# Expert weights of an encoder layer in one ring of fourteen 1 MB slots, loaded in order of use

## The reference

```python
h = h + memory_cross_attention(rms_norm(h, norm_cross[l]), mem_n, xa_wq[l], xa_wk[l], xa_wv[l], xa_wo[l])
h = h + hierarchical_moe(rms_norm(h, norm_ffn[l]), moe_router_group[l], moe_router_expert[l],
                         moe_w1[l], moe_w3[l], moe_w2[l])
return rms_norm(h, norm_final)

def expert_block(args):                     # for each expert, on the tokens routed to it
    xblk, e = args
    return (jax.nn.silu(xblk @ w1[e]) * (xblk @ w3[e])) @ w2[e]
```

## Time and profile before

| | us |
|---|---|
| median of 3 runs | 1872.28 |
| the profiled execution, its own time | 1873.4 |
| its span, first to last instruction | 1871.6 |
| PE busy in it | 1724.3 |

### The profile page before, as it was taken

How to read it: one execution, slowest core, us unless ns; L and a number is a source line. 1 busy time by engine, 2 the same in 40 slices (tenths; PEclk the granted TensorE clock), 3 DMA queues, 4 the chain that set the end, 5 groups by cost and what they waited for, 6 DMA issues and landing times.

```text
span 1871.6 us, 26055 instructions
## 1 busy us (share of the span) xinstructions
PE 1724.3 (92%) x10706; PEld 1088.5 (58%) x10706; DVE 840.5 (45%) x1165; ACT 522.3 (28%) x747; POOL 64.8 (3%) x33
## 2 busy tenths in 40 slices
PE   7989999999999999999799988899888898988996
PEld 7879899899777899978543332233323233232332
DVE  5566555798666454354643232232322323232233
ACT  5453443644354453344411000011000110000102
POOL 0004000033000000000000000000000000000001
PEclk9999999999999999999899999999999999999998
DMA  8753645444455565338499999999999999999995
GB/s 325 253 178 106 223 159 179 148 153 143 150 176 180 182 193 177 116 135 315 166 402 423 427 427 428 428 429 428 428 428 429 428 429 428 429 428 429 428 428 229
DMA packets 105393, 561.03 MB, mean 300 GB/s; under 512 B 9696, under 2 KB 9824, under 8 KB 79200
## 3 DMA queue, kind: packets, MB, share of 16 engines
q1 hardware_dynamic: 95808, 436.13, 59.7%
q10 hardware_dynamic: 9504, 123.74, 15.7%
HBM read 557.75 MB, written 2.10 MB: 299 GB/s over the span
## 4 chain that ended last, share of the span: by engine, by line
PE 67%; DMA 27%; DVE 3%; ACT 1%; issue 1%; SPq 0%; ACTq 0%; DVEq 0%
DMA arena<-in_moe_w_dram 27%; PE ps L970 14%; PE ps L617 7%; PE ps L619 6%; PE ps L618 6%; PE ps L611 6%; PE ps L612 6%; PE ps L613 6%; PE ps L1000 5%; PE ps L982 2%; PE ps L1017 2%; PE ps L916 1%; DVE w_lo L1575 1%; PE ps L858 1%; PE ps L839 1%
## 5 line engine op out<-in xcount | busy, mean ns | idle before, releaser
L970 PE MATMUL ps<-arena 128*64 128x512 f32 x2048 | 504.6, 627 | 84.1 <-DMA arena<-in_moe_w_dram 82.5
L1575 DVE TENSOR_TENSOR w_lo<-arena,w_hi 128x1024 fp32r<-128x1024 f32 x264 | 331.4, 1297 | 237.8 <-ACT w_hi L1145 237.6
L1145 ACT ACTIVATE w_hi<-arena 128x1024 fp32r<-128x1024 f32 x264 | 265.1, 1054 | 309.3 <-PE ps L613 169.4
L970 PEld LDWEIGHTS ps<-arena 128*64 128x64 f32 x2048 | 138.1, 142 | 346.4 <-issue 252.9
L2200 DVE TENSOR_TENSOR arena<-ps,arena 128x1024 f32<-128x1024 f32 x128 | 156.7, 1225 | 274.0 <-PE ps L1017 274.0
L1000 PE MATMUL ps<-arena 128*64 128x512 f32 x1024 | 225.6, 593 | 5.2 <-DVE arena L2177 3.2
L611 PE MATMUL ps<-x_hi,w_hi 128*128 128x256 f32 x512 | 148.4, 290 | 19.0 <-DVE w_lo L1575 19.0
L1000 PEld LDWEIGHTS ps<-arena 128*64 128x64 f32 x1024 | 73.2, 137 | 149.3 <-issue 139.5
L612 PE MATMUL ps<-x_lo,w_hi 128*128 128x256 f32 x512 | 147.5, 288 | 0.0
L613 PE MATMUL ps<-x_hi,w_lo 128*128 128x256 f32 x512 | 147.4, 288 | 0.0
L1430 ACT ACTIVATE arena<-ps 128x512 f32<-128x512 f32 x64 | 38.3, 599 | 385.3 <-PE ps L970 385.3
(11 more groups left out here) (363 smaller groups left out, 2409.7 us busy)
## 6 DMA issues: line engine op xcount, KB each, us to landing
arena<-in_moe_w_dram SPq DMA_DIRECT2D x133, 2048.0 KB, 20.1
arena<-in_moe_w_dram ACTq DMA_DIRECT2D x58, 2048.0 KB, 14.1
arena<-in_w_in_dram SPq DMA_DIRECT2D x52, 1024.0 KB, 5.1
arena<-in_xa_wk_dram SPq DMA_DIRECT2D x16, 1024.0 KB, 5.0
arena<-in_xa_wv_dram SPq DMA_DIRECT2D x16, 1024.0 KB, 5.0
arena<-in_w_out_dram SPq DMA_DIRECT2D x16, 1024.0 KB, 5.0
arena<-in_xa_wq_dram SPq DMA_DIRECT2D x16, 1024.0 KB, 5.0
arena<-in_xa_wo_dram SPq DMA_DIRECT2D x16, 1024.0 KB, 5.2
```

The source lines that it names most:

```text
L970: last = mm(ps[rows_, m, :], xe[par][:, ECH * i + c, :], ring_up[m][i][:, c, :], start=(i == 0 and c < 2), stop=(i == ECH - 1 and c >= 2))
L1145: fn(hi_ring[(2 * n + u) % 4][:], ring_a[i][:, 2 * u:2 * u + 2, :], ACT.Copy).then_inc(S["w_hi"], 1)
L1575: V.tensor_tensor(w_lo[i][:, 2 * u:2 * u + 2, :], ring_a[i][:, 2 * u:2 * u + 2, :], hi_ring[(2 * n + u) % 4][:].bitcast(F32), ALU.subtract ...
```

## The change

It replaces the three areas by one ring of 14 slots of 1 MB. `load_order` lists all 384 pieces in the order in which PE uses them; piece k goes to slot k mod 14 and waits only until piece k-14 is used. Two slots are new (`extra`, 16 KB of each partition; the scratch of the software DMA queue is cut to 1024 bytes to make room). All loads are of one piece, 8 KB for each partition, and all are on SP's queue; ACT issues none. Fourteen pieces can be loaded before the first is used: the 8 ups of expert 0, two ups of expert 1, the 4 downs of expert 0.

In the last column group of the output projection, PE finishes tokens 0 to 127 first (`last_stream`, `last_turn`, `last_logits`), and the add, squares, root and `hx_hi` of each half go on as soon as that half is there. `low_tokens` is cut finer. On PE two ups of expert 1 stand ahead of `slot_rows`, and the wait for the tables (`tab_dve`) goes to the end; the second half of the gather moves from experts 1 and 2 to experts 2 and 3. On DVE `tokens(1)` stands ahead of `select` of the second half and the tables. PE's and SP's loops over experts are written out. The core of the diff:

```diff
-RING_E = 3 * ECH
+UNIT = 1
+IN_PARTS = ()
...
+def load_order():
+
+    order = []
+    for n in range(NE + 1):
+        ups = [(n, m, i) for m in range(2) for i in range(0, ECH, UNIT)] if n < NE else []
+        downs = [(n - 1, 2, i) for i in range(0, ECH, UNIT)] if n else []
+        ahead = 2 // UNIT if 0 < n < NE - 2 else 0 if n else len(ups)
+        order += ups[:ahead] + downs + ups[ahead:]
+    return order
...
+        extra = Arena(sb("extra", [P, 16 * 256]))
...
-        ring_kib = [104, 112, 120, 128, 152, 160, 184, 192, 136, 144, 168, 176]
-        ring_up = [[arena(ring_kib[ECH * m + i], ECH, FF) for i in range(ECH)] for m in range(2)]
-        pair_up = [[arena(ring_kib[ECH * m + i], 2 * ECH, FF) for i in (0, 2)] for m in range(2)]
-        pair_dn = [arena(ring_kib[2 * ECH + i], 2, D) for i in (0, 2)]
-        ring_dn = [arena(ring_kib[2 * ECH + i], D) for i in range(ECH)]
+        slot_kib = [kib + 8 * k for kib in (104, 120, 152, 184, 202, 136, 168) for k in range(0, 2, UNIT)]
+        order = load_order()
+        unit_of = {unit: at for at, unit in enumerate(order)}
+        loads = [0] * len(slot_kib)
+        landed = []
+        for at in range(len(order)):
+            loads[at % len(slot_kib)] += 2 if at in IN_PARTS else 1
+            landed.append(loads[at % len(slot_kib)])
...
+
+        def slot_of(n, m, i):
+
+            first = i - i % UNIT
+            return unit_of[(n, m, first)] % len(slot_kib) if isinstance(n, int) and n < NE else over_slot[(m, first)]
+
+        def piece(n, m, i, many=1):
+
+            kib = slot_kib[slot_of(n, m, i)] + 8 * (i % UNIT)
+            home, kib = (arena, kib) if kib < 202 else (extra, kib - 202)
+            return home(kib, many * ECH, FF) if m < 2 else home(kib, many, D) if many > 1 else home(kib, D)
...
-            def load_up(e, n, m, i):
-
-                if not (isinstance(n, int) and n == 0):
-                    sp.wait_ge(S["up_used0" if m == 0 else "up_used1"], n * ECH + (i + 2 - ECH))
-                sp.dma_start(pair_up[m][i // 2], up_chunk(e, m, i)).then_inc(s_up[m][i // 2], 16)
-
-            def load_down(e, i):
-
-                sp.dma_start(pair_dn[i // 2], down_chunk(e, i)).then_inc(s_dn[i // 2], 16)
-
-            def load_expert(e, n):
-                for m in range(2):
-                    for i in range(0, ECH, 2):
-                        load_up(e, n, m, i)
+            used = ("up_used0", "up_used1", "dn_used")
+
+            def load_unit(at):
+
+                n, m, i = order[at]
+                parts, many = (2, 1) if at in IN_PARTS else (1, UNIT)
+                for k in range(parts):
+                    if at >= len(slot_kib):
+                        was_n, was_m, was_i = order[at - len(slot_kib)]
+                        sp.wait_ge(S[used[was_m]], was_n * ECH + was_i + (k + 1 if parts == 2 else UNIT))
+                    sp.dma_start(piece(n, m, i + k, many), expert_rows(n, m, i + k, many)).then_inc(s_slot[at % len(slot_kib)], 16)
...
             for m in range(2):
                 load_dense(G_XO + 2 + m)
-                for i in range(0, ECH, 2):
-                    load_up(0, 0, m, i)
+                for at in range(4 * m // UNIT, 4 * (m + 1) // UNIT):
+                    load_unit(at)
+            for at in range(8 // UNIT, 10 // UNIT):
+                load_unit(at)
...
+            def last_stream(j, i):
+
+                g, (a_hi, a_lo) = G_XO + 3, split[G_XO]
+                n_split, hi_ring = split_chunk(g, i)
+                o_, rows_ = ps[:, 2 * (g % 2) + j, :], slice(j * P, (j + 1) * P)
+                for c in range(CH):
+                    k, half = i * CH + c, 2 * n_split + c // 2
+                    if j == 0 and c % 2 == 0:
+                        pe.wait_ge(S["w_lo"], half + 1)
+                    hi, lo = hi_ring[half % 4][:, c % 2, :], w_lo[i][:, c, :]
+                    mm(o_, a_hi[:, k, rows_], hi, start=False, stop=False)
+                    mm(o_, a_hi[:, k, rows_], lo, start=False, stop=False)
+                    last = mm(o_, a_lo[:, k, rows_], hi, start=False, stop=(k == KT - 1))
+                if j == 1:
+                    last.then_inc(S["chunk_used"], 1)
+                elif i == NCH - 1:
+                    last.then_inc(S["xo_half"], 1)
+
+            def last_turn(j):
+
+                if j == 0:
+                    pe.wait_ge(S["proj_a"], act_evicts(G_XO + 4))
+                    pe.wait_ge(S["tp_act"], 3)
+                    pe.wait_ge(S["tp_dve"], 3)
+                else:
+                    pe.wait_ge(S["proj_b"], G_XO + 4)
+                for kk in (6, 7):
+                    for u in range(2):
+                        k = 2 * kk + u
+                        last = nc.tensor.transpose(bank(4 + kk % 2, 2, NT, P)[:, u, j, :], h[:, j, k * P:(k + 1) * P], ident)
...
-                dense_split(G_XO + n, False, split[G_XO], part=[2, 3])
-            group_turned(G_XO, 3, turn, 0)
-            logits(3)
-
-            pe.wait_ge(S["route_in"], 16)
+                if n < 3:
+                    dense_split(G_XO + n, False, split[G_XO], part=[2, 3])
+            last_stream(0, 2)
+            last_stream(0, 3)
+            last_stream(1, 2)
+            last_turn(0)
+            last_stream(1, 3)
+            last_logits(0)
+            last_turn(1)
+            last_logits(1)
...
+            up(1, 0, 0, 1)
+            up(1, 0, 1, 1)
             slot_rows()
-            pe.wait_ge(S["tab_dve"], 2)
-            block_n(1, 0, 1, (0, 1))
-            block_n(2, 1, 0, (2, 3))
-            block_n(3, 2, 1)
-            block_n(4, 3, 0)
-            block_n(5, 4, 1)
-            with pe.Fori(0, NE // 2 - 4) as e:
-                block_n(e * 2 + 6, e * 2 + 5, 0)
-                block_n(e * 2 + 7, e * 2 + 6, 1)
+            sums(0)
+            up(1, 0, 2, 1)
+            for i in range(ECH):
+                down(0, i)
+            up(1, 0, 3, 1)
+            for i in range(ECH):
+                up(1, 1, i, 1)
+                comb(0, i, 0)
+            for n in range(2, NE - 2):
+                block_n(n, n - 1, n % 2, {2: (0, 1), 3: (2, 3)}.get(n, ()))
             block_n(NE - 2, NE - 3, 0, behind=True)
             block_n(NE - 1, NE - 2, 1, behind=True)
             finish_n(NE - 1, 1)
+            pe.wait_ge(S["tab_dve"], 2)
...
+            act.wait_ge(S["proj_a"], act_evicts(G_XO + 4))
+            act.wait_ge(S["sq_part"], 6)
+            part_square(3, 0)
             sqrt_table()
-            rsqrt(NT)
-            act.wait_ge(S["rms_dve"], 2)
-            for j in range(NT):
-                fn(hx_hi[:, j], h[:, j, :].rearrange("p (q k) -> p k q", k=KT), ACT.Copy,
-                   scale=st[:, 40 + j:41 + j]).then_inc(S["hx_act"], 1)
+            root_of(0)
+            last_turned(0)
+            act.wait_ge(S["chunk_used"], (G_XO + 4) * NCH)
+            normalised(0)
+            act.wait_ge(S["proj_b"], G_XO + 4)
+            act.wait_ge(S["sq_part"], 7)
+            part_square(3, 1)
+            last_turned(1)
+            root_of(1)
+            normalised(1)
...
-            def down_hi(n, load):
-                for i in range(0, ECH, 2):
-                    act.wait_ge(S["dn_used"], n * ECH + i + 2)
-                    if load is not None:
-                        act.dma_start(pair_dn[i // 2], down_chunk(load, i)).then_inc(s_dn[i // 2], 16)
+            def down_hi(n):
+                act.wait_ge(S["dn_used"], n * ECH + ECH)
...
+            dve.wait_ge(S["xo_half"], 1)
+            last_add(0)
+            variance_of(0)
+            V.memset(lgrp, LOWEST)
+            last_turned(0)
+            inverse_of(0)
+            dve.wait_ge(S["chunk_used"], (G_XO + 4) * NCH)
+            last_add(1)
             V.memset(onesm, 1.0)
-            V.memset(lgrp, LOWEST)
-            dve.wait_ge(S["sq_part"], 8)
-            step(V.tensor_reduce(st[:, 0:NT], st[:, 44:52].rearrange("p (j g) -> p j g", g=4), AX.X, ALU.add))
-            rsqrt(NT, 1.0 / D)
-            V.tensor_copy(st[:, 40:42], st[:, 24:26]).then_inc(S["rms_dve"], 1)
+            last_turned(1)
+            variance_of(1)
+            inverse_of(1)
+            dve.wait_ge(S["rms_dve"], 3)
...
+            tokens(1, start_of(1), 1)
...
-            block_n(0, 0, 0, True, (0, 1))
-            block_n(1, start_of(1), 1, True, (2, 3))
-            dve.wait_ge(S["g_dve"], 8)
-            block_n(2, start_of(2), 0, True)
+            block_n(0, 0, 0, True)
+            block_n(1, start_of(1), 1, True, (0, 1))
+            block_n(2, start_of(2), 0, True, (2, 3))
```

More of the change, by code:

```diff
@@ L1391, in part_square @@
                 fn(arena(88, 512), h[:, j, GW * n:GW * (n + 1)], ACT.Square, accum_out=st[:, 44 + 4 * j + n:45 + 4 * j + n]).then_inc(S["sq_part"], 1)
-            for n in range(5):
+            for n in range(4):
                 if n < 4:
@@ L1446, in down_hi, with block_n @@
                     fn(d_hi[u][:], ps[:, 4 + u, :], ACT.Copy).then_inc(S["ev_hi"], 1)
```

(37 more changed lines are left out.)

162 lines of the change are left out of this document (84 added, 78 removed).

## The result

The changed kernel takes **1880.8 us** (median of 6 runs, 1879.2 to 1882.6) against 1872.5 us before (6 runs beside it, 1871.5 to 1874.4). The ratio is 1.0039, with a 95% interval from 1.0028 to 1.0049: **slower by 0.4%**. The forecast was 1862.0 us in a range from 1857 to 1875, so both the sign and the range were wrong. The profiled execution took 1881.4 us with a span of 1879.6, 8.0 us more than the one of before.

A forecast was written before the change was run, and what follows sets the result against it. DMA loads of expert weights at 428 GB/s were taken to bound the expert part, with gaps at the front. 1873.4 - 7.4 (with the router's 0.3 in it) - 2.9 = 1863.1, less 1.1: 1862.0 us, range 1857 to 1875.

The forecast's parts named there:

- Step 5: Long stream of expert loads: 1 MB in 1 MB loads with 8 KB runs still takes 2.45 us, cost 0.
- step 2: Start of the expert part: fourteen slots and single pieces put loads 3.0 MB ahead, -7.4 us (bounds -4.9 and -9.3).
- step 4: End of the expert part: last down ends 1.9 us behind the last landing, where before it was 4.8; -2.9 us.
- Rival A: Expert loads: runs have a price, +13 us, giving 1875.0 us, no change that can be measured; chance 0.20.
- B: Expert loads: each load has its own price, which doubling the loads doubles; slower, 1884 us at 0.06 per MB; chance 0.14.
- Step 3: Queues: SP's 384 issues at 0.33 us are hidden; ACT's fewer issues, PE's moved wait and later gather cost nothing.
- Step 1: Router by token halves, ahead of the gather: net +0.3 us, at least -3, at most +1.5; gather starts at 914.0.
- rival D: Front: the router by halves gains 3 us, or the loss from 950 to 1000 us goes: 1859 us; chance 0.10.
- Rival C: Start of the expert part: first downs come late, at 952 and not 948.3 us, giving 1865.7 us; chance 0.07.

The follow-up runs named there:

- the mix: Kernel with the ring in 2 MB loads, its gate and up loads from expert 1 on in 4 KB runs, downs kept at 16 KB: 1897.9 us, ratio 1.0124.

## Why the prediction was wrong

**Step 5 failed**, the price of 1 MB in loads of 1 MB with 8 KB runs. It took 0 and the rows say 0.041 us for each MB, 14.0 us. Of the 18.3 us between the sum's 1863.1 and the 1881.4 of the profiled execution it is 14.0; step 2 is 1.7, the tail 0.9, step 4 0.3 and 1.4 rounding and code. Against the same ring with 16 KB runs (427.53 GB/s by its packets) the runs alone are 0.038 for each MB, 13 us. Its own bound for a price per run, worked out from dense loads of 2 KB runs, was just that: 0.036 and 13 us. The two rows that it was given up for can't carry it. A loss of 1.7% is 0.04 us in the 2.5 between two last landings, which are read to a tenth. And the window of 4 us with 8 KB runs at 428 GB/s is no better: five windows of 2 us in the old kernel, from 1830 to 1840 us, read anything from 410 to 438. Rival A had the mechanism, at 0.20, and the mark of 422 GB/s; it came out at 1875 only because its base carried the steps below. The trace shows 421, between the marks of A (422) and B (below 421), so the mark alone does not decide, but the run with 8 KB runs in 2 MB loads refutes B: it has as many loads as the kernel without the loss.

The 408.7 GB/s of the Trainium skill (DMA: Bandwidth & Descriptors, section iDMA fabric — 4 AXI ports for 8 engines, asymmetric across TPBs), which the prediction gave to a price for each load, fits a price for each run: 4 KiB rows are 256 + 16 packets to the MB, 200 more than 16 KB runs, and 200 x 0.6 ns on 2.450 are 2.57 us, which is that rate. It is an estimate, since no run here had all its bytes in such rows; the mix measured 415. The rule of SBUF — State Buffer in the Trainium skill (section The DMA setup-cost knee), the largest single transfer, pointed the right way, but the size of the transfer is not what the runs here show to matter.

**Step 2 was too large** as a sum, and undervalued the slots themselves. Against the -7.4 stand -5.7, 2.3 MB ahead and not 3.0: the last dense matmul ended 1.7 us later in this execution (899.09, and 897.38 before), 0.4 of it for the transposes that now stand ahead, and 950 to 1000 us gave 407 GB/s, less again than the 412 that it left as they were. The slots by themselves are worth 9.5 us, about its bound of 9.3 for this step.

**Step 3 failed in part.** It put the rearrangement of areas and queues at nothing. At twelve slots the ring, with the halves and the rows moved, costs 6 to 7 us against the old kernel, of which the halves and the rows are about 1 each at most. Nor did it price the written-out loops of PE and SP: by the traces their code accounts for the longer tail and for up to 2.5 us of the stream. Its price of 0.33 us for an issue was wrong (2.1 us of SP with eleven loads outstanding, and SP shows with 2% in the chain), but issues are hidden all the same, and neither one queue nor two matters.

**Step 1 was about right**: gathers at 914.79 for a forecast of 914.0. From the end of the last dense matmul they come 15.7 us later, 16.4 before, so the step gained 0.7 where a loss of 0.3 was forecast, and 0.4 of it are transposes moved ahead. The reason is the one that it gave: `hx_hi` of the first half, ahead of the squares, costs what the halves gain. The 3 us that rival D hoped for are there once it is moved (3.0 measured, 2.1 by the ratios).

**Step 4 was right**: -2.6 for -2.9, the downs end 2.2 behind the last landing for a forecast of 1.9. The tail of the DMA engines, 0.9, was not foreseen. Rival C didn't come: the first downs start at 949.03.

By parts, from the ratios: ring at twelve slots about +6, two more slots -9.5, loads of 1 MB +10.9 (the runs +13 and 2.7 back at the end). The expected gain of the slots was real and was paid out again through the length of a run.

## What to carry to other kernels

Where the DMA engines are the limit, count runs and not only bytes: cutting a load in two by columns of a partition's row doubles its runs, and 0.5 to 0.6 ns for each run outweighed here what finer slots bring. Halve loads only where it pays, at the end or at the front, and keep long runs in between; with 2 MB loads and the squares first the same ring takes 1867.2 us, below both kernels. Program code is loaded beside the weights: before a loop is written out beside a stream that limits the kernel, look at the packets of code in the page. A difference of 2% in a rate can't be read from two landings or a window of 4 us: take the bound from the far row, or leave both ends in the sum.

## What the runs showed of the hardware

- The price of a run is the same from 16 to 8 KB and from 8 to 4 KB, 0.49 to 0.64 ns by the rates of four kernels, whatever the size of the load or the number of queues: 428, 421 and 415 GB/s at 72, 136 and 200 packets to the MB (421 and 422 at 144, in loads of 1 MB).
- A run is one packet up to 32 KB: 31 loads of 128 runs of 32 KB in place of 62 of 128 of 16 KB made 4464 packets fewer, 144 for each, which is 128 runs and 16 more.
- A packet of 16 KB of program code takes one DMA engine 1.07 us, one of weights 0.61. In every kernel with the ring, where such code comes about once in 26 us, half of the DMA engines end some 6 us behind the others (share 0.5); in the old one, with loops, it was 2 us. That the one makes the other is read from the traces, not tested.
- With eleven loads of 1 MB outstanding an issue takes SP 2.13 us and not 0.33 (medians; single ones up to 7.2), and 2.4 with 2 MB loads of 8 KB runs; the rate does not follow it.
